# Two of the four weight sums of each seven-product set: from VectorE adds to accumulating transfers on GpSimd's queue

## The reference

```python
def _squared_relu_mlp(x, w1, w2):
    h = jax.nn.relu(x @ w1)
    return (h * h) @ w2
...
u = jnp.square(jax.nn.relu(h @ w_ff1[l] + b_ff1[l]))
ffn_out = u @ w_ff2[l] + b_ff2[l]
```

## Time and profile before

| | value |
|---|---|
| median of 3 runs | 2011.74 us (2011.65 to 2012.68) |
| profiled execution | 2011.64 us, span 2009.9 us |
| TensorE matmuls (PE), busy | 1988.7 us, 99% of the span |
| TensorE weight loads (PEld), busy | 1745.1 us, 87% |
| VectorE (DVE) busy | 1244.9 us, 62% |
| ScalarE (ACT) busy | 930.5 us, 46% |
| GpSimd (POOL) busy | 175.8 us, 9% |
| moved by transfers | 220.26 MB, mean 110 GB/s |

### The profile page before, as it was taken

The page is one execution under the profiler, slowest core; times in us unless marked ns, Lnnn a source line. Parts: engine busy times, 40 slices in busy tenths (PEclk is TensorE's granted clock), DMA queues, the critical chain, the costliest instruction groups (busy, mean ns, idle before and its releaser), DMA issues.

```text
span 2009.9 us, 30736 instructions
## 1 busy us (share of the span) xinstructions
PE 1988.7 (99%) x12508; PEld 1745.1 (87%) x12508; DVE 1244.9 (62%) x1928; ACT 930.5 (46%) x1546; POOL 175.8 (9%) x162
## 2 busy tenths in 40 slices
PE   9999999999999999999999999999999999999998
PEld 7888898889898888889798999987888898989897
DVE  6557767766476646537874666738544545757474
ACT  7425655444363533323552535535554436445262
POOL 1001011000001002212200003300000210000000
PEclk9999999999999999999999999999999999999999
DMA  5222012444352322222253443232112213445341
GB/s 196 80 76 72 23 54 95 147 147 167 116 179 74 126 95 84 84 94 89 102 177 116 168 147 126 98 105 93 53 64 84 95 53 111 157 136 173 120 163 42
DMA packets 62396, 220.26 MB, mean 110 GB/s; under 512 B 6976, under 2 KB 9168, under 8 KB 62256
## 3 DMA queue, kind: packets, MB, share of 16 engines
q1 hardware_dynamic: 60432, 210.98, 30.6%
q0 software_dynamic: 1824, 7.32, 1.0%
HBM read 216.18 MB, written 2.10 MB: 109 GB/s over the span
## 4 chain that ended last, share of the span: by engine, by line
PE 91%; DVE 5%; ACT 2%; issue 1%; DMA 0%; POOL 0%; SPq 0%; ACTq 0%; DVEq 0%
PE ps L503 40%; PE ps L1009 18%; PE ps L1413 5%; PE ps L584 4%; PE ps L2083 3%; PE ps L2160 3%; PE ps L623 3%; PE ps L1353 2%; PE ps L1396 2%; PE ps L1370 1%; PE ps L2173 1%; PE ps L1782 1%; PE ps L938 1%; DVE ring L476 1%; PE ps L1919 1%; PE ps L2071 1%
## 5 line engine op out<-in xcount | busy, mean ns | idle before, releaser
L476 DVE TENSOR_TENSOR ring<-raw,ring 128x1024 fp32r<-128x1024 f32 x374 | 473.1, 1271 | 175.8 <-ACT ring L451 171.0
L451 ACT ACTIVATE ring<-raw 128x1024 fp32r<-128x1024 f32 x374 | 388.2, 1051 | 321.1 <-DVE raw L463 187.0
L503 PE MATMUL ps<-xb,ring 128*128 128x512 f32 x2208 | 504.8, 390 | 1.7 <-DVE xb L1242 1.7
L503 PEld LDWEIGHTS ps<-xb,ring 128*128 128x128 f32 x2208 | 414.0, 188 | 88.8 <-DVE xb L1242 2.1
L503 PE MATMUL ps<-xa,ring 128*128 128x512 f32 x1320 | 308.3, 392 | 0.2 <-DVE ring L476 0.2
L503 PEld LDWEIGHTS ps<-xa,ring 128*128 128x128 f32 x1320 | 246.1, 188 | 51.7 <-issue 1.3
L1009 PE MATMUL ps<-xa,ring 128*128 128x256 f32 x1728 | 211.7, 283 | 0.0
L1009 PEld LDWEIGHTS ps<-xa,ring 128*128 128x128 f32 x1728 | 209.9, 192 | 0.7
L1009 PE MATMUL ps<-n,ring 128*128 128x256 f32 x1296 | 160.6, 284 | 0.3
L1009 PEld LDWEIGHTS ps<-n,ring 128*128 128x128 f32 x1296 | 157.3, 192 | 2.0 <-DVE ring L476 1.2
L1256 DVE TENSOR_TENSOR acc<-acc,ps 128x512 f32<-128x512 f32 x68 | 46.8, 688 | 177.3 <-PE ps L503 177.3
(11 more groups left out here) (406 smaller groups left out, 2497.2 us busy)
## 6 DMA issues: line engine op xcount, KB each, us to landing
raw<-in_stream SPq DMA_DIRECT2D x374, 512.0 KB, 3.2
other<-in_stream SPq DMA_DIRECT2D x18, 512.0 KB, 4.5
t<-in_rpb POOLq DMA_DIRECT2D x8, 384.0 KB, 5.1
h<-in_x SPq DMA_DIRECT2D x8, 256.0 KB, 7.2
c_w<-in_cmp_w POOLq DMA_DIRECT2D x4, 512.0 KB, 4.5
out_y<-h SPq DMA_DIRECT2D x10, 128.0 KB, 1.8
out_y<-h SPq DMA_DIRECT2D x3, 256.0 KB, 2.2
cons<-in_con SPq DMA_DIRECT2D x1, 578.0 KB, 9.2
```

The source lines that it names most:

```text
L451: nc.scalar.activation(ring[:, at_slot, 0], raw[:, at_slot, 1], ACT.Copy).then_inc(hi_done, 1)
L476: nc.vector.tensor_tensor(ring[:, at_slot, 1], raw[:, at_slot, 1], ring[:, at_slot, 0].bitcast(F32), ALU.subtract).then_inc(lo_done, 1)
L503: mm = nc.tensor.matmul(bank[:, :], ring[:, SLOT[n], w, k * P:(k + 1) * P], operand[:, k, xx], start=(start and i == 0 and w == 0 and xx = ...
```

## The change: what it does

Number 1 and number 4 of each set are no longer summed by VectorE. The panel still lands in its slot by SyncE's load. A new function `pool_pairs` lets GpSimd wait for that landing and then issue a second transfer from the stream in DRAM into the same slot, tile 21 of the set, with addition: what is in the slot is read, the tile is added, and the sum is written back. Its landing is counted by `pair_in0` (number 1) or `pair_in1` (number 4). ScalarE's hi of these two panels waits for that count, and so does VectorE's add that makes number 2 from number 1. The staging buffer and its load on SyncE's queue are gone; tile 21 is now read twice per set.

```diff
--- before.py
+++ after.py
@@ -85,7 +85,8 @@
 
 SET_LANDS = ("11", "22", "11", "12", "11", "12", "22")
 SET_ADDS = (None, "21", 1, 2, "21", None, None)
-SET_SUM = (None, 1, 2, 3, 4, None, None)
+SET_SUM = (None, None, 1, 2, None, None, None)
+SET_PAIR = {1: 0, 4: 1}
 SET_TURN = (0, 1, 2, 4, 3, 5, 6)
 TILE = ("11", "12", "21", "22")
 SET_BANK = (0, 2, 1, 3, 1, 0, 3)
@@ -350,7 +351,6 @@
         lneps = at("lneps", [P, T], 56)
         gained = at("gained", [P, T], 58)
         quads = at("quads", [P, 4, T], 48)
-        other = at("other", [P, 2, KC * P], 72)
         n1, n1f = (nc.alloc_sbuf_tensor_at(name, [P, 4, 2, HT], dt, offset=xf_at) for name, dt in (("n1", F32R), ("n1f", F32)))
         n2, n2f = (at(name, [P, 4, 2, HT], 56, dt) for name, dt in (("n2", F32R), ("n2f", F32)))
         n3, n3f = (at(name, [P, 4, 2, HT], 64, dt) for name, dt in (("n3", F32R), ("n3f", F32)))
@@ -436,7 +436,7 @@
             at = set_of(m)
             if at is None or SET_SUM[at[1]] is None:
                 return None
-            return 4 * at[0] + SET_SUM[at[1]]
+            return 2 * at[0] + SET_SUM[at[1]]
 
         def act_split(act, n):
 
@@ -444,8 +444,11 @@
             if m >= NP:
                 return
             at_slot = SLOT[m]
+            at = set_of(m)
             if summed(m) is not None:
                 act.wait_ge(sem("set_sums"), summed(m))
+            elif at is not None and at[1] in SET_PAIR:
+                act.wait_ge(sem(f"pair_in{SET_PAIR[at[1]]}"), 16 * (at[0] + 1))
             else:
                 act.wait_ge(landed[m % RING], 16 * (m // RING + 1))
             nc.scalar.activation(ring[:, at_slot, 0], raw[:, at_slot, 1], ACT.Copy).then_inc(hi_done, 1)
@@ -454,12 +457,11 @@
 
             d, i = set_of(n)
             dve.wait_ge(landed[n % RING], 16 * (n // RING + 1))
-            if SET_ADDS[i] == "21":
-                dve.wait_ge(sem(f"other_in{d % 2}"), 16 * (d // 2 + 1))
-                more = other[:, d % 2]
+            if SET_ADDS[i] in SET_PAIR:
+                dve.wait_ge(sem(f"pair_in{SET_PAIR[SET_ADDS[i]]}"), 16 * (d + 1))
             else:
                 dve.wait_ge(sem("set_sums"), summed(n - i + SET_ADDS[i]))
-                more = raw[:, SLOT[n - i + SET_ADDS[i]], 1]
+            more = raw[:, SLOT[n - i + SET_ADDS[i]], 1]
             nc.vector.tensor_tensor(raw[:, SLOT[n], 1], raw[:, SLOT[n], 1], more, ALU.add).then_inc(sem("set_sums"), 1)
 
         def dve_split(dve, n):
@@ -1119,6 +1121,17 @@
             first, d = set_at(s, g, u)
             dve.wait_ge(panel_done, first + 7)
             nc.vector.tensor_tensor(quads[:, 0], ps[4 * u + 3][:, :], quads[:, 0], ALU.subtract).then_inc(sem("set_sum"), 1)
+
+        def pool_pairs(pool, s):
+
+            for g in range(1, GROUPS):
+                for u in range(2):
+                    first, d = set_at(s, g, u)
+                    for i in SET_PAIR:
+                        n = first + i
+                        pool.wait_ge(landed[n % RING], 16 * (n // RING + 1))
+                        pool.dma_start(raw[:, SLOT[n], 1], stream[SET_SRC[d] + TILE.index("21")], accum_op=ALU.add)\
+                            .then_inc(sem(f"pair_in{SET_PAIR[i]}"), 16)
 
         GAINS = {"ffn0": 2, "ffn1": 6}
 
@@ -1621,13 +1634,6 @@
                     sp.wait_ge(panel_done, TURN[BEFORE[n]] + 1)
                 sp.wait_ge(landed[n % RING], 16 * (n // RING))
                 sp.dma_start(raw[:, SLOT[n], 1], stream[SRC[n]]).then_inc(landed[n % RING], 16)
-                at = set_of(n)
-                if at is not None and at[1] == 0:
-                    d = at[0]
-                    if d >= 2:
-                        sp.wait_ge(sem("set_sums"), 4 * (d - 1))
-                        sp.wait_ge(sem(f"other_in{d % 2}"), 16 * (d // 2))
-                    sp.dma_start(other[:, d % 2], stream[SET_SRC[d] + TILE.index("21")]).then_inc(sem(f"other_in{d % 2}"), 16)
             for k in range(KC):
                 sp.wait_ge(sem("y_ready"), k + 1)
                 sp.dma_start(out[:, k, half(0)], h[:, k, half(0)]).then_inc(sem("stored"), 16)
@@ -1688,6 +1694,7 @@
                         nc.gpsimd.tensor_tensor(part[:, half(s)], xf[:, 0, 0:HT] if 2 * q + c == 1 else part[:, half(s)],
                                                 xf[:, q, half(c)], ALU.add).then_inc(sem("post_part"), 1)
             pool_squares(pool, 1)
+            pool_pairs(pool, "ffn0")
             pool_post_full(pool, 1)
             for s in range(2):
                 for q in range(3):
@@ -1719,6 +1726,7 @@
                     .then_inc(sem("post_part"), 1)
             pool_base_sum(pool)
             pool_squares(pool, 2)
+            pool_pairs(pool, "ffn1")
             pool_post_full(pool, 3, lambda k: pool_gain_part(pool, k))
             for q in range(3):
                 pool_post_half(pool, 3, 0, q)
@@ -1755,6 +1763,7 @@
                             pool_ln_lo(pool, m, s, k)
 
             pool_ln(1, "mix2_out", h, True)
+            pool_pairs(pool, "ffn2")
             pool_ln(2, "ffn2", acc, False)
 
         @block.tensor
```

## The result

The changed kernel takes 2049.71 us (median of 4 runs, 2048.44 to 2052.75) where the kernel before took 2011.89 beside it: ratio 1.0189, interval [1.0172, 1.0207]. It is slower, as forecast, but by 38 us and not by 5, and so it lies above the range, which ended at 2036.

What follows compares the result with a forecast made beforehand. TensorE, busy 99%, was taken as the bound, waiting 2.0 us for VectorE at number 4. At t = 6.3 late sums add 1.8 + 1.8 + 1.45 = 5.1 us to 2011.64: forecast 2017 us, range 2009.6 to 2036.

Steps and rivals of the forecast that it cites:

- The 2.0 us as the most that VectorE's relief can give back: TensorE's idle time at product number 4 of nine second sets, 2.0 us in all, caps the gain from 36 fewer adds.
- First sets free: In the pairs' first sets the room allows t = 8.6 from panel landing to sum landing, so no cost at 6.3.
- Staging load and GpSimd's own load at nothing: Dropping SyncE's 18 loads of `other` gains nothing; GpSimd runs nothing else in the sets, so issuing transfers costs nothing.
- t, one value for all second sets, 6.3: Panel landing to sum landing, taken as 6.3 us; at number 4 of nine second sets it costs 5.1 us.
- the middle price, t = 5.7: Sums landing 5.7 us after their panels, in time for TensorE, would give a kernel time of 2011.3 us.
- The panel's landing as a fixed 3.1 us after its issue: Number 4's panel in ffn1's second set, issued at 1032.05, was taken to land 3.1 us later, at 1035.15.
- my own formula: At number 4 of nine second sets, each 0.1 us of t above the mean 5.74 costs 0.9 us of kernel time.
- This wait decides nothing before t = 6.9: Number 2's add waiting for number 1's sum costs nothing below t = 6.9, then adds to number 4's stall.
- The sign in the DMA issues: Median landing time of GpSimd's 36 transfers: about 6.1 us by the forecast, under 5.6 if in time, over 7 if much slower.
- the case without a loss: Rival: sums at numbers 1 and 4 land in time, t up to 6.1, 2009.6 to 2015 us; chance 38%.
- Much slower: Rival: adding transfers exceed what two reads explain and slow loads beside them, t from 7.2, 2025 to 2052 us; chance 17%.
- The rule on two source reads: Skill rule: adding transfers need two source reads, 1.93 times a copy; applied to landing time, 6.6 us and 2021 us total.

Runs made afterwards that it cites:

- The last experiment: Kernel before, with VectorE's lo of the hidden activations moved behind number 4's lo in second sets: 2011.17 us, ratio 0.9992.
- two plain tiles: Changed kernel with each adding transfer replaced by a plain 1 MB transfer into a staging buffer, sums missing: 2044.95 us, ratio 1.0163 to the kernel before.
- the kernel with both numbers held: Changed kernel, but second sets' loads of numbers 2 and 5 wait for the transfers of 1 and 4: 2049.83 us, ratio 1.0188 to the kernel before.
- number 1 alone: Kernel before, with only number 1 summed by adding transfer in all sets, number 4 by VectorE: 2028.06 us, ratio 1.0059.
- first sets alone: Kernel before, with adding transfers for numbers 1 and 4 only in each pair's first set (18 transfers): 2017.30 us, ratio 0.9996.

## Why the prediction was too low

- **The 2.0 us as the most that VectorE's relief can give back: right.** The last experiment takes them without moving any add. VectorE's 39 us instead of 44 are no error of count: an add began up to 0.09 us before the instruction ahead had ended, and the next one before the add had the earlier trace rows, and busy time counts overlaps once.
- **First sets free: right.** Their sums land 5.4 to 5.9 us after the panel, against 8.6 allowed; TensorE loses nothing. The loads issued beside these transfers did take 4.1 to 6.5 us, but nothing stood on them.
- **Staging load and GpSimd's own load at nothing: right.** None of it shows.
- **t, one value for all second sets, 6.3: the step that failed.** In first sets t is 5.4 to 5.9, so the middle price, t = 5.7, would have followed from a transfer that the loads leave alone (priced at 2011.3 us there; with the gain of six sets ending at 0.2 us each, as the prediction itself has it, 2011.9). In the second sets it is 6.3 to 9.5 for number 1 (mean 7.8) and 5.6 to 9.0 for number 4 (mean 7.4). I read a row of three transfers side by side as if it were a property of the adding transfer, when t depends on what else is under way: held apart from the loads, the same transfers take 5.1 to 5.6 us in second sets too. The mean share was 57% before, and I took that for room; over the 8.6 us behind number 1's issue it is 86%.
- **The panel's landing as a fixed 3.1 us after its issue: failed with it.** In the set shown it became 6.3, because number 1's transfer was still under way. Measured from its landing, number 4's t alone would have given (7.4 - 5.74) x 9 = 15 us by my own formula, which is what the way from product 2 to number 4 gained (14.9, with part of the slow clock in it). That this fits is luck: the nine panels landed 1.7 us later than before on average (5.1 us after their issue instead of 3.4), and TensorE came to number 4 that much later too, by its 15.5 us at products 1 and 2.
- **"This wait decides nothing before t = 6.9": the threshold was about right, its conclusion not.** In the kernel before, number 2's add could have come 6.7 us after number 1's landing without delay. But number 1's transfer took up to 9.5, and products 1 and 2 lost 15.5 us that the sum had at zero. The prediction names idle time at another place than number 4 as its sign of a wrong mechanism, and that is what happened.
- **The sign in the DMA issues: misleading.** The median time to landing of the 36 transfers is 5.4 us, which the prediction had put down to the case without a loss. Half of the 36 are those of first sets, and the median hides the other half.
- **The clock: not foreseen.** Some 7 us.
- **The rivals.** "Much slower" had the mechanism, loads slowed as well, and its bounds 2025 to 2052 hold the result; I gave it 17% and said that nothing in the rows spoke either way. Its number for t = 8.4, 2036, had the same fault as the forecast: it stretched number 4's transfer only. Its reason, that read, add and write back follow each other, is not needed for such a loss: two plain tiles bring the same.
- **The rule on two source reads.** The engines' time for an adding transfer is 51 us to a plain one's 26, a ratio of 1.97. The Trainium skill's 1.93 ("Collectives: The Full Stack", section "The bandwidth ceiling: the fold count and why AG ≠ RS ≠ AR") agrees with that. I had applied it to the time to landing, 6.6; a lone one lands in 5.4, since not all of the landing time is engine time. Engine time is where the rule fits here.

## What to carry to other kernels

Before a copy is replaced by an adding transfer, take its time to landing beside the loads that will run with it, not alone (7.3 us against 5.3 here), and compare that with the room; in engines' time an add counted as two transfers of its size here (51 us against 26). The mean share of a long stretch tells neither. A transfer that is put in series between a load and its consumer lengthens the loads beside it as well, so the room must be counted for those too. Where such a transfer has to stay, hold back the loads that aren't needed yet, and only those.

## What was not expected of the hardware

- The granted clock fell to 0.50 in or behind stalls of 2.2 to 4.1 us. In the kernel with both numbers held, with 33.6 us of idle time on the sets' line but none over 2.1 us at once, one stretch of 3.4 us at 0.50 lies in the sets; with number 1 alone, 17.2 us and none over 1.8, none does. Such stretches come outside the sets too: with first sets alone there are two, behind stalls of 1.9 and 4.1 us.
- A plain transfer of two tiles landed as late as an adding one of one tile, 5.4 us each, and disturbed the loads as much.
- In the trace's packet records of the set shown, 15 of the 16 shares of number 1's addition were done by 1043.3 (each share closes with a packet of 4 bytes); the last took until 1047.4, its pieces 0.48 us apart. The landing is that of the last share. It is not this set alone: in seven of the nine second sets twelve shares of number 1's transfer were done 4.7 to 4.9 us after its issue, as in first sets, and the last at 5.7 to 8.9; for number 4 the picture is mixed. So number 1's late landing there is not an even slowing of all engines, which a sum over 16 of them would suggest. Why a few lag is open.
